# Stick-breaking attention's row sums: one float32 triangle product per head against two float32r products on a split of the logs

## What is computed

```python
z = jnp.einsum('bqhd,bkhd->bhqk', qblk, k).astype(jnp.float32) * scale
log_beta = jax.nn.log_sigmoid(z)
log_keep = jnp.where(strict, log_beta - z, 0.0)
after = lax.cumsum(log_keep, axis=3, reverse=True) - log_keep
a = jnp.where(strict, jnp.exp(log_beta + after), 0.0)
return jnp.einsum('bhqk,bkhd->bqhd', a.astype(v.dtype), v)
```

## Time and profile before

| | |
|---|---|
| median of 3 runs | 488.03 us (487.99 to 489.65) |
| the profiled execution | 487.81 us |
| its span | 486.1 us |
| busy: PE, PE weight load, VectorE, ScalarE, GpSimd | 470.4, 302.0, 239.2, 176.0, 6.5 us |
| chain that ended last, share of PE | 93% |
| branch C's sums on PE, first and last start | 96.3 and 127.1 us |

### The profile page before, as it was taken

How to read it: one execution, slowest core, us unless ns; L and a number is a source line. 1 busy time by engine, 2 the same in 40 slices (tenths; PEclk the granted TensorE clock), 3 DMA queues, 4 the chain that set the end, 5 groups by cost and what they waited for, 6 DMA issues and landing times.

```text
span 486.1 us, 7868 instructions
## 1 busy us (share of the span) xinstructions
PE 470.4 (97%) x3253; PEld 302.0 (62%) x3253; DVE 239.2 (49%) x395; ACT 176.0 (36%) x263; POOL 6.5 (1%) x19
## 2 busy tenths in 40 slices
PE   7999999999999999999999999999999999999992
PEld 6997998878788888888886534433334242433331
DVE  5858766667648366484458731240315040404034
ACT  5645654685794173246173310110112011100104
POOL 4010000000000000000000000000000000000000
PEclk9999999999999999999998999999999999999997
DMA  8996576422542990865769499999999999999962
GB/s 283 387 283 255 175 295 225 174 93 81 174 161 86 409 382 0 296 223 214 305 245 424 165 423 422 419 386 421 394 423 421 422 375 426 423 419 423 419 261 87
DMA packets 37615, 144.58 MB, mean 297 GB/s; under 512 B 4552, under 2 KB 7248, under 8 KB 25296
## 3 DMA queue, kind: packets, MB, share of 16 engines
q1 hardware_dynamic: 37584, 144.14, 75.6%
HBM read 143.09 MB, written 1.05 MB: 297 GB/s over the span
## 4 chain that ended last, share of the span: by engine, by line
PE 93%; DVE 3%; DMA 2%; ACT 1%; issue 0%; SPq 0%; DVEq 0%; ACTq 0%
PE bank L1735 34%; PE bank L1491 32%; PE bank L1478 11%; PE bank L1726 3%; PE bank L1746 3%; DMA ring<-in_w_in 2%; PE bank L1589 1%; PE bank L1700 1%; PE bank L1810 1%; PE bank L1693 1%; DVE x_lo L915 1%; ACT gate L866 1%; PE bank L1576 1%; PE bank L1603 0%; DVE work L1394 0%; DVE ring_lo L890 0%
## 5 line engine op out<-in xcount | busy, mean ns | idle before, releaser
L1735 PE MATMUL bank<-ring,work 128*32 128x512 f32 x1280 | 140.9, 593 | 2.2 <-ACT work L842 2.2
L1735 PEld LDWEIGHTS bank<-ring,work 128*32 128x32 f32 x1280 | 39.9, 110 | 91.9 <-issue 89.4
L890 DVE TENSOR_TENSOR ring_lo<-ring,w_hi 128x2048 fp32r<-128x2048 f32 x38 | 86.2, 2284 | 20.0 <-ACT w_hi L644 20.0
L644 ACT ACTIVATE w_hi<-ring 128x2048 fp32r<-128x2048 f32 x37 | 70.3, 1911 | 53.8 <-DMA ring<-in_w_in 27.3
L1394 DVE SCALAR_TENSOR_TENSOR work<-bank,st,work 128x512 f32<-128x512 f32 x8 | 9.1, 1137 | 67.9 <-PE bank L1735 67.9
L1491 PE MATMUL bank<-w_hi,x_hi 128*128 128x512 f32 x144 | 39.4, 396 | 0.0
L1491 PE MATMUL bank<-w_hi,x_lo 128*128 128x512 f32 x144 | 38.6, 390 | 0.0
L1491 PE MATMUL bank<-ring_lo,x_hi 128*128 128x512 f32 x144 | 38.5, 389 | 0.0
L1491 PEld LDWEIGHTS bank<-w_hi,x_lo 128*128 128x128 f32 x144 | 27.0, 188 | 5.7
L1491 PEld LDWEIGHTS bank<-ring_lo,x_hi 128*128 128x128 f32 x144 | 27.0, 188 | 5.7
L1491 PEld LDWEIGHTS bank<-w_hi,x_hi 128*128 128x128 f32 x144 | 26.4, 188 | 6.1 <-issue 0.8
(11 more groups left out here) (284 smaller groups left out, 580.8 us busy)
## 6 DMA issues: line engine op xcount, KB each, us to landing
ring<-in_moe_w SPq DMA_DIRECT2D x80, 1024.0 KB, 11.3
ring<-in_w_in SPq DMA_DIRECT2D x13, 2048.0 KB, 8.8
late_slot<-in_moe_w SPq DMA_DIRECT2D x16, 1024.0 KB, 15.2
ring<-in_w_out SPq DMA_DIRECT2D x2, 2048.0 KB, 11.0
ring<-in_w_in SPq DMA_DIRECT2D x2, 1024.0 KB, 8.9
ring<-in_w_up_b SPq DMA_DIRECT2D x1, 2048.0 KB, 8.7
ring<-in_w_up_c SPq DMA_DIRECT2D x1, 2048.0 KB, 7.4
ring<-in_w_up_a SPq DMA_DIRECT2D x1, 2048.0 KB, 9.1
```

The source lines that it names most:

```text
L644: act.activation(hi(q), raw(q), ACT.Copy).then_inc(w_hi_ready, 1)
L890: dve.tensor_tensor(lo(q), raw(q), hi(q).bitcast(F32), ALU.subtract).then_inc(w_lo_ready, 1)
L1735: ins = pe.matmul(bank[cols, dst, :], lhsT[:, k, first + j * STRIP:first + (j + 1) * STRIP], rhs[e][:, k, :], start=(k == 0), stop=(k == n ...
```

## The change

`from_here` becomes a float32r tile. For each head VectorE makes, behind the addition that ended `c_keep`, a rounded copy `sp_hi` of the logs and the rest `sp_lo = diff - sp_hi`, each waiting for the step before by a new semaphore `c_split`; `c_sp` is now signalled by the last of the three. The two parts lie in the room of `xn`, which holds nothing at that time. PE multiplies the triangle with each of the two in float32r. The product with `ones` on the last 128 columns stays float32 and reads `diff`.

```diff
-        from_here = at("from_here", [P, P], LATE + 20 * W3, F32)
+        from_here = at("from_here", [P, P], LATE + 20 * W3)
+
+        sp_hi = at("sp_hi", [P, 2, W3], X2)
+        sp_lo = at("sp_lo", [P, 2, W3], X2 + 8 * W3)
...
-        c_abs = sem("c_abs")
+        c_abs, c_split = sem("c_abs"), sem("c_split")
...
                 dve.scalar_tensor_tensor(out=w, in0=prob[:, h % 4, :], scalar=0.0, in1=w,
-                                         op0=ALU.max, op1=ALU.add).then_inc(c_sp, 1)
+                                         op0=ALU.max, op1=ALU.add).then_inc(c_split, 1)
+
+                dve.wait_ge(c_split, 2 * h + 1)
+                dve.tensor_copy(sp_hi[:, h % 2, :], diff[:, h % 2, :]).then_inc(c_split, 1)
+                dve.wait_ge(c_split, 2 * h + 2)
+                dve.tensor_tensor(sp_lo[:, h % 2, :], diff[:, h % 2, :], sp_hi[:, h % 2, :].bitcast(F32),
+                                  ALU.subtract).then_inc(c_sp, 1)
...
-                pe.matmul(b[:, 0:W3], from_here[:, :], w, start=True, stop=False, skip_group_check=True)
+                for part in (sp_hi, sp_lo):
+                    pe.matmul(b[:, 0:W3], from_here[:, :], part[:, h % 2, :], start=(part is sp_hi), stop=False,
+                              skip_group_check=True)
                 pe.matmul(b[:, P:T], ones[:, :], w[:, T:W3], start=False, stop=True, skip_group_check=True)\
                   .then_inc(c_summed, 1)
```

## The result

| | before | changed |
|---|---|---|
| median, six runs of each on one chip | 489.61 us (487.99 to 490.23) | 492.98 us (491.7 to 494.68) |
| profiled execution | 487.81 us | 491.7 us |
| its span | 486.1 us | 490.0 us |
| branch C stretch: first score product of heads 0 and 1 to first gates product | 38.02 us | 41.40 us |

The ratio is 1.0078, with an interval of 1.0052 to 1.0103, so the change costs 2.5 to 5.0 us; the medians are 3.37 apart. The forecast was 3.4. So the measured time lies in the range that was named (489.4 to 494.2), but not between the forecast's own bounds (491.1 to 492.6).

A forecast was written before the change was run, and what follows sets the result against it. The prediction took PE's stream as the bound, with the VectorE and ScalarE loop hardly ahead of it. Head 7's 3.62 us delay - 0.295 saved + 0.1 restart gave 3.4 us, so 491.4 us, range 489.4 to 494.2.

The forecast's parts named there:

- the forecast's own bounds: Low and high ends of the split's and products' costs: 3.1 to 4.6 us slower, 491.1 to 492.6 us.
- What bounds the kernel: Branch C: PE's stream, busy 97% of the span, sets the end; the VectorE and ScalarE loop is hardly ahead.
- PE's saving: Each head's triangle on PE takes 0.35 us in place of 0.65, saving 0.295, or 2.4 for eight heads.
- VectorE's cost: Copy 0.38, subtraction 0.555 and waits 0.08 make each head's c_sp 1.015 us later; VectorE is busy 8.1 us longer.
- The sum: At head 7: PE 3.62 us late, less 0.295 saved, plus 0.1 for restarting, gives 3.4 us.
- second version of the sum: At head 7, with one float32r pass at 0.65 / 4 us, the sum would be 3.37 us.
- Round by round: Branch C's four rounds: each adds its split, so additions of heads 3, 5, 7 come 1, 2, 3 us later.
- The waits: PE waits for VectorE's subtraction in rounds 1 to 3, some 5 us in about six waits, where none was.
- The rival of a lost round: Slack between 94 and 106 us absorbs one round's delay: 2.4 us slower, 490.4 us; chance 0.14.
- The rival of the float32r pass: Each float32r part on PE takes 0.65 us like the float32 product: 493.9 us; chance 0.05.
- The rival of the covered split: Additions have enough lead every round, so PE only gains: 2.4 us faster, 485.7 us; chance 0.05.
- The rival of the clock: PE's stalls around 107, 118 and 128 us make the granted clock fall: 1.7 us more, 493.1 us; chance 0.10.

The follow-up runs named there:

- e2: Changed kernel without the split: VectorE's addition writes rounded logs, PE multiplies them twice in float32r; stretch 37.49 us (-0.53 against before), time ratio 0.9998.
- e4: Kernel before, with two of VectorE's weight subtractions moved behind the logits; stretch 37.94 us (-0.08 against before), time ratio 0.9992.
- e5: e2 with the two weight subtractions moved behind the logits; stretch 36.31 us (-1.71 against before), time ratio 0.9967.
- e7: Changed kernel with VectorE's copy into sp_hi made twice in a row for each head; stretch 44.28 us (+6.26 against before), time ratio 1.0135.
- e1: Changed kernel with the split kept but PE's product float32 as before; stretch 41.59 us (+3.57 against before), time ratio 1.0075.
- e3: Changed kernel with two of VectorE's weight subtractions moved behind the logits; stretch 41.13 us (+3.11 against before, clock fell), time ratio 1.0001.
- e9: The kernel of e3 profiled once more; stretch 39.74 us (+1.72 against before, clock fell), one execution of 488.7 us.

## Why the prediction was right

- *What bounds the kernel.* The forecast rested on reading PE's 97% together with the loop behind it. e2 shows that PE's share alone misleads (0.53 of 2.4 us), and e4 that the loop alone misleads as well: the two were equal. Both together, e5, give 1.71.
- *PE's saving.* 0.295 us a head was the term; 0.87 - 0.57 = 0.30 was measured. It is shared out otherwise than forecast: the triangle takes 0.43 us in place of 0.64 (97.13 to 97.56, before 96.27 to 96.91), not 0.35, and the product with ones behind it 0.14 in place of 0.23, where the forecast had it stay. That the two add up to the term is luck.
- *VectorE's cost.* Copy 0.38, measured 0.36; subtraction 0.555, measured 0.559; two hand-overs of 0.04, measured 0.04 (94.85 + 0.56 to 95.45). A head has 0.98 to 0.99 in all, where the forecast had 1.015. VectorE's busy time grew by 7.4 us, not by 8.1, which had the waits in it. The Trainium skill, "VectorE: DVE Perf Modes", in its TRN2 errata table, has 0.26 for the copy and 0.46 for the subtraction by its fixed terms. A head would be 0.80 by that, and the sum 2.6 (an estimate from the page; the forecast has 2.5); the measured rows decide against it. The Trainium skill says in the same section that this row is too low; its formula for a float32 tensor_tensor there, (N + 151) / 0.96, gives 0.557 us for 384 columns (an estimate), and the trace agrees with that, 0.559.
- *The sum.* Head 7's sums start 3.48 us late (130.81 - 0.94 - 126.39), not 3.62, since a split is a little cheaper than forecast. From there to the product with ones PE takes 0.46 us in place of 0.65, which is the forecast's -0.295 + 0.1. Then the copy L945 adds the 0.09 that the forecast put at nothing. 3.48 - 0.19 + 0.09 = 3.38: the mechanism is as forecast, but that the sum fits to a few hundredths is luck, for two errors of some 0.1 us cancel. Two smaller slips of the forecast change nothing: its second version of the sum, with 0.65 / 4 us for a pass, comes to 3.40 by its own terms, not 3.37, and its rival without the single pass to 493.8, not 493.9.
- *Round by round.* Later by 1, 2 and 3 us at heads 3, 5 and 7, said the forecast; 1.0, 1.9 and 2.9 were measured, and e7 moved them on by another 0.7 a round when the split was made 0.4 longer.
- *The waits.* "Some 5 us in about six waits", measured 4.3 in six. The 2.1 us that PE saves beside the last head go there. e1, which doesn't save them, has nearly the same stretch. It is 0.19 longer: head 7's products take 0.29 more there (0.75 to 0.46 from their start to the product with ones), and the 0.09 of the copy falls away.
- *The rival of a lost round* falls with the additions' times. *The rival of the float32r pass* falls with the records of 0.34 us. *The rival of the covered split* falls with e1.
- *The rival of the clock* is half right. The changed kernel's profile has 1.00 throughout the stretch, though PE was busy only 2.10 of 4 us from 106 to 110:

```profile
106.00:110.00 4.00, 2.10 (x13) 1.67 (x14) 3.25 (x8) 3.90 (x9) 0.00 (x0) 1.00 0.94 311
```

But of the five profiles in which PE waited 1.9 us or more for VectorE in this stretch (changed, e1, e3, e7, e9), three show the lower level behind such waits, and none of the others does. So the forecast's 0.10 for a fall looks too low for any one execution. Where it came in an execution of the changed kernel, it would have been hidden in part, as in e7, by the loop that was late anyway. Some of the six timed executions (491.7 to 494.7 us) may have had it: four of them have a mean granted clock of 0.983, and none of the 71 of before that were timed beside the experiments has less than 0.986. Where in the kernel they lost it, no row shows.

The Trainium skill, "TensorE: Matmul & The Clock Gate", Part 1, has the gate go down when the array is not busy enough; the rows of e3, e7 and e9 agree that waits between wide products can do it, not only narrow products as in the router. In e7 the pair of waits behind which it fell (1.24 and 1.01 us) was the shorter one: behind 1.62 and 1.01 us a round earlier it stayed at 1.00. What decides between a fall and none stays open.

## What to carry to other kernels

Before a product on a busy engine is made cheaper by work on an engine that looks half idle, follow the loop that this engine is in, and compare the time at which its last result lands with the time at which the busy engine takes it, round by round. A cost in such a loop is paid once a round, and carried, and more than once where the other head's no longer hides (e7); here 1.0 us a round made 3.4 us out of an engine that was 49% busy. The same account says what to do: subtractions of 2.3 us that nobody was waiting for stood in the loop's way, and moving two of them gave back what the change had cost, as far as the time can tell (1.0001, 0.9976 to 1.0026). It gave no gain over the kernel before: no version with the whole computation was clearly faster than that.

## What was not expected of the hardware

The granted clock fell to the lower of its two levels behind waits of 0.7 to 1.2 us between products of 384 and 256 columns, in three profiles of five, and for different times: by the rows of 1 us, 3.4 us in e9 and e7 and 6.8 in e3. In e3 and e9 that cost 2.9 and 1.5 us of the stretch; in e7, nothing. In e3 and e7 the clock then stayed at 1.00 through the router, where it fell in the other ten profiles. Whether the one has to do with the other, two profiles don't show.
